# Score, value and up products of a two-block network: the order in which a matmul visits its moving columns

## The reference

```python
def peer_ffn(h, ...):                       # first block, 16384 experts, 8 heads
    ...                                     # routing: the 16 best experts of each head, and their gates
    def chunk(args):
        hc, ec, gc = args
        u = peer_u[ec]
        a = jax.nn.gelu(jnp.einsum("ckd,cd->ck", u, hc)) * gc
        vv = peer_v[ec]
        return jnp.einsum("ck,ckd->cd", a, vv)

def second_block(...):
    ...
    up = causal_dwconv(h2 @ w_up[l], ffn_conv_w[l], ffn_conv_b[l])     # w_up is 1024 x 6144
    gate_h, val_h = jnp.split(up, 2, axis=-1)
    x = x + (jax.nn.gelu(gate_h, approximate=True) * val_h) @ w_down[l]
```

## Time and profile before

| | |
|---|---|
| median of the runs | 1597.97 us |
| the runs | 1597.45 and 1598.48 us |
| span of the profiled execution, first to last instruction | 1595.2 us |
| TensorE matmul busy (PE) | 1583.0 us, 99% |
| weight loads busy (PEld) | 1493.5 us, 94% |
| VectorE, ScalarE, GpSimd busy | 1071.3, 884.2, 885.8 us |
| mean granted TensorE clock | 0.999 |
| DMA | 277.03 MB, mean 174 GB/s |

### The profile page before, as it was taken

One profiled execution on the slowest core, in us unless ns is written; L12 is line 12 of the kernel. 1 busy time (PEld: TensorE's weight loads), 2 busy tenths in 40 slices (PEclk: granted clock), 3 DMA queues, 4 the chain that ended last, 5 costly groups with the idle time before them and its releaser, 6 DMA issues.

```text
span 1595.2 us, 33476 instructions
## 1 busy us (share of the span) xinstructions
PE 1583.0 (99%) x12568; PEld 1493.5 (94%) x12568; DVE 1071.3 (67%) x1867; ACT 884.2 (55%) x1251; POOL 885.8 (56%) x413
## 2 busy tenths in 40 slices
PE   9999999999999999999999999999999999999998
PEld 8999899999999999998888888889999999999998
DVE  7998643779933777778888666776937383455521
ACT  6557766454454444444444445457676654666653
POOL 8786468868886000000000244457876689888886
PEclk9999999999999999999999999999999999999999
DMA  6565346555555555555555666666543356666653
GB/s 222 171 191 154 106 132 187 186 175 190 188 184 186 171 171 171 172 169 171 179 178 166 215 190 194 195 189 185 172 148 106 109 177 185 188 190 187 191 187 119
DMA packets 86218, 277.03 MB, mean 174 GB/s; under 512 B 11233, under 2 KB 18161, under 8 KB 86129
## 3 DMA queue, kind: packets, MB, share of 16 engines
q1 hardware_dynamic: 85712, 274.76, 54.9%
q0 software_dynamic: 272, 1.05, 0.2%
q10 hardware_dynamic: 144, 0.00, 0.0%
HBM read 274.73 MB, written 1.05 MB: 173 GB/s over the span
## 4 chain that ended last, share of the span: by engine, by line
PE 93%; issue 2%; DVE 2%; POOL 1%; ACT 1%; DMA 0%; SPq 0%; DVEq 0%; ACTq 0%; POOLq 0%
PE gemm L679 36%; PE gemm L982 22%; PE gemm L684 18%; PE aux L1268 4%; PE gemm L813 3%; PE aux L962 2%; POOL w_lo L462 1%; PE gemm L700 1%; PE gemm L725 1%; PE gemm L1268 1%; PE aux L932 0%; PE gemm L799 0%; ACT w_hi L1364 0%; PE gemm L706 0%; PE gemm L742 0%
## 5 line engine op out<-in xcount | busy, mean ns | idle before, releaser
L462 POOL TENSOR_TENSOR w_lo<-raw,w_hi 128x1024 fp32r<-128x1024 f32 (+1 forms) x330 | 791.7, 2407 | 294.7 <-ACT w_hi L1364 285.6
L1364 ACT ACTIVATE w_hi<-raw 128x1024 fp32r<-128x1024 f32 (+1 forms) x492 | 515.8, 1050 | 575.5 <-PE gemm L679 324.0
L679 PE MATMUL gemm<-h_lo,w_hi 128*128 128x256 f32 x2144 | 294.3, 279 | 0.0
L679 PE MATMUL gemm<-h_hi,w_hi 128*128 128x256 f32 x2096 | 293.3, 282 | 0.4 <-ACT w_hi L1364 0.3
L684 PE MATMUL gemm<-h_hi,w_lo 128*128 128x256 f32 x2096 | 288.6, 280 | 1.4 <-POOL w_lo L462 0.9
L679 PEld LDWEIGHTS gemm<-h_lo,w_hi 128*128 128x128 f32 x2144 | 268.9, 188 | 0.3 <-issue 0.2
L679 PEld LDWEIGHTS gemm<-h_hi,w_hi 128*128 128x128 f32 x2096 | 264.0, 188 | 3.3 <-issue 1.6
L462 DVE TENSOR_TENSOR w_lo<-raw,w_hi 128x1024 fp32r<-128x1024 f32 x162 | 196.6, 1222 | 104.3 <-ACT w_hi L1364 103.7
L684 PEld LDWEIGHTS gemm<-h_hi,w_lo 128*128 128x128 f32 x2096 | 262.8, 188 | 3.5 <-POOL w_lo L462 2.2
L982 PE MATMUL gemm<-w_hi,act_parts 128*128 128x512 f32 x1008 | 250.9, 391 | 0.4 <-ACT act_parts L1565 0.4
L982 PEld LDWEIGHTS gemm<-w_hi,act_parts 128*128 128x128 f32 x1008 | 188.0, 188 | 39.0 <-issue 0.5
(11 more groups left out here) (436 smaller groups left out, 2065.6 us busy)
## 6 DMA issues: line engine op xcount, KB each, us to landing
raw<-in_w_u SPq DMA_DIRECT2D x128, 512.0 KB, 3.6
raw<-in_w_ev SPq DMA_DIRECT2D x128, 512.0 KB, 3.7
raw<-in_w_up SPq DMA_DIRECT2D x48, 512.0 KB, 4.3
raw<-in_w_gate SPq DMA_DIRECT2D x24, 512.0 KB, 3.8
raw<-in_w_down SPq DMA_DIRECT2D x24, 512.0 KB, 4.0
raw<-in_w_conv_in SPq DMA_DIRECT2D x16, 512.0 KB, 4.6
raw<-in_w_peer_q SPq DMA_DIRECT2D x16, 512.0 KB, 3.5
raw<-in_w_branch SPq DMA_DIRECT2D x24, 288.0 KB, 2.9
```

The lines of the kernel that those rows point to most:

```text
L462: eng.tensor_tensor(w_lo[v][:, 0:n], raw[c.raw][v][:, 0:n], w_hi[v][:, 0:n], ALU.subtract).then_inc(lo_ready[v], 1)
L679: mm = pe.matmul(out, w[:, k, :], act_part[:, k, :], start=(n == k == 0), stop=False)
L1364: act.activation(w_hi[v][:, 0:n], raw[c.raw][v][:, 0:n], ACT.Copy).then_inc(hi_ready[v], 1)
```

## The change

Four new things stand ahead of the products. `ordered(tile, groups, run)` cuts the columns into `groups` equal stretches and visits a run of `run` columns from each stretch in turn. `strided(tile, groups, run)` visits every `groups`-th run first, then the ones behind them, and so on. A run is never shorter than 4 columns, which is 16 bytes. `column_order(c)` finds the order of a chunk by its name and its place in the round, and gives back the columns unchanged for every other chunk. `turn` is put around the moving operand and the output of the matmul alike, so that each column still gets its own sum.

```diff
+        def ordered(tile, groups, run):
+            if groups == 1:
+                return tile
+            return tile.rearrange("p (g j c) -> p j g c", g=groups, c=run)
+
+        def strided(tile, groups, run):
+            return tile.rearrange("p (j g c) -> p g j c", g=groups, c=run)
+
+        SCORE_ORDER = (lambda x: x, lambda x: ordered(x, 2, 4), lambda x: strided(x, 2, 4), lambda x: ordered(x, 2, 8))
+        VALUE_ORDER = (lambda x: ordered(x, 2, 4), lambda x: ordered(x, 4, 4), lambda x: ordered(x, 2, 16), lambda x: x)
+        UP_ORDER = (lambda x: ordered(x, 4, 8), lambda x: ordered(x, 2, 64), lambda x: ordered(x, 8, 4), lambda x: strided(x, 4, 4))
+
+        def column_order(c):
+            for name, orders in (("u", SCORE_ORDER), ("up", UP_ORDER), ("ev", VALUE_ORDER)):
+                first = plan[name][0].index
+                if first <= c.index < first + len(plan[name]):
+                    return orders[(c.index - first) % BANKS]
+            return lambda x: x
@@ product_tile
+                turn = column_order(c)
...
-                        mm = pe.matmul(out, w[:, k, :], act_part[:, k, :], start=(n == k == 0), stop=False)
+                        mm = pe.matmul(turn(out), w[:, k, :], turn(act_part[:, k, :]), start=(n == k == 0), stop=False)
...
-                    mm = pe.matmul(out, w[:, k, :], x[0][:, k, :], start=False, stop=(k == steps - 1))
+                    mm = pe.matmul(turn(out), w[:, k, :], turn(x[0][:, k, :]), start=False, stop=(k == steps - 1))
@@ expert_values
+                turn = column_order(c)
...
-                                mm = pe.matmul(gemm[2 * half + tt][:, :], a[:, c.raw, v, tt * P:(tt + 1) * P],
-                                               w[v][:, half * (D // 2):(half + 1) * (D // 2)],
+                                mm = pe.matmul(turn(gemm[2 * half + tt][:, :]), a[:, c.raw, v, tt * P:(tt + 1) * P],
+                                               turn(w[v][:, half * (D // 2):(half + 1) * (D // 2)]),
```

## The result

The changed kernel takes 1645.23 us (1644.97 and 1645.49) against 1597.97: ratio 1.0296, 95% interval 1.0279 to 1.0314. That is 47.3 us slower, where I had forecast 6 us faster.

The account below looks back on a forecast made before the run. TensorE, always busy, bounds the kernel: matmul distance times number of matmuls. Changes of distance at the turned places summed to -6.1 us, from 1595.2 to 1589.1, plus 2.8 us around the span: forecast 1592 us, range 1575 to 1655.

Parts of the forecast that it names:

- no cover was used up: In u, GpSimd needs 4.84 us for a chunk's remainders, of 5.6 us, so TensorE's gain or loss arrives whole.
- I take zero for a jump: In all turned places a jump inside the columns costs nothing; at 1.67 ns, 281 thousand jumps would cost 469 us.
- The meetings with the weight load: In float32r matmuls, moving stream and weight load wanting one 128-byte residue cost 1.67 ns; four now, 6.7 ns.
- my ten terms: Changes of matmul distance at the turned places of u, ev and up, counted in meetings; sum -6.1 us.
- u's place 2: In u, every second group, then the others: about 6 meetings against four, +3.3 ns x 768, +2.6 us.
- up's place 2: In up, eight stretches in turn, all of one residue: 6 meetings, +3.3 ns x 288, +1.0 us.
- Up's place 3: In up, every fourth group: 8 meetings, +6.7 ns, +1.9 us; it should be the slowest in up.
- the four pairs: Operand pairs in u, query product and by_token (twice): 116 to 118.8 ns by their place difference modulo 128 bytes.
- Order doesn't matter: All turned products: stalls come from how fast float32r columns are read, weights shift them 1.5 ns; 1598 us, chance 0.27.
- the in-step rival: u's and ev's halves in turn, 4 columns, always meet the weights: 28 meetings more, +46.7 ns, above 1653 us; chance 0.08.
- A residue twice in a row: In u, ev and up, groups following one of their own residue pay 1.67 ns each: +171 us, 1769 us; chance 0.10.
- The output: Turned products: jumping writes into PSUM fall to half rate, 217 and 433 ns a matmul, +583 us, 2181 us; chance 0.03.

Follow-up runs that it names:

- the bare streams: Separate kernels computing nothing of the reference: TensorE alone runs streams of 32 matmuls with nothing to wait for; contiguous 256 columns took 116.7 ns each.
- one order for all: Kernel before the change, with each fourth group of 16 bytes in every product of 256 moving columns, value products as they lie: 1580.3 us, ratio 0.988.

## Why the prediction was wrong, point by point

- What bounds the kernel: right. PE was full before and after, the clock stood at its upper level, no wait came in, and the loss is the number of matmuls times the growth of their distance.
- The change adds no instruction and no wait, and no cover was used up: right. The count of matmuls is the same, TensorE's waits are those of before, and the run without the value orders comes out at the sum.
- **"I take zero for a jump"**: this is the step that failed. The reason given was that a contiguous stream changes its 16-byte group as often. It is the distance to the next group that has a price. Halves in turn, 4 columns, have 64 jumps for 10.0 ns, so 0.16 ns each, 128 for 23.7 in ev, 0.19; four stretches in ev 0.32 each; ev's place 2 with 32 jumps 0.42. These lie between my two bounds, 0 and 1.67, and I set the sum at the lower one; only every 4th group in up, with 64 jumps for -1.8 ns, lies below it. In all, the 281 thousand jumps that I had counted at nothing came with 48 us.
- **The meetings with the weight load**: wrong as the source of the sum. Of my ten terms two have the right sign and a size within 6 ns (u's place 2 and up's place 2); the others miss by sign or kind. Up's place 3, which I had as the slowest of up, was the only one that got faster. The reading of the earlier trace rows holds within this kernel: over the whole trace the four pairs stand 117.0, 118.1, 118.5 and 117.0 ns apart. As a rule it fell, because in the bare streams 114.0 and 118.3 ns have the same difference of 112 bytes. And I took all 8 ns of extra for such meetings. With a quarter of the weight columns a contiguous stream still takes 116.6 to 120.0 ns, so most of them are not.
- "Order doesn't matter" fell, and with it the Trainium skill's rule in "TensorE: Matmul & The Clock Gate", Part 2, in its strict form. The weight load does act on the moving stream: 64 bytes past the weights a matmul takes 113.3 ns with 128 weight columns and 120.0 with 32, eight stretches in turn 127.2 and 116.7, and with both operands on one residue it takes 240 ns where 217 is the least.
- The measured time lies in my range of 1575 to 1655 us by luck. What reached above 1600 was the in-step rival with its chance of 0.08; to a slower kernel I had given 0.21 in all. That rival gave 1653 us, near to the 1645 measured, but not for its reason: it has +46.7 ns in u's place 1 and ev's place 0 and nothing in ev's place 1, which paid the most.
- A residue twice in a row: fell as priced, with eight stretches in turn and 32 weight columns (116.7 ns). The turned places whose neighbours are of one residue did pay, but for halves in turn 0.16 ns each and not 1.67.
- The output: fell, output alone is 1602 us. The slowing that the Trainium skill gives for any non-contiguous pattern in "PSUM — Partial Sum Buffer", Specifications (TRN2), didn't show for runs of four columns or more: with the output alone turned, bare streams took 116.7 to 117.8 ns, contiguous 116.7.
- The rule of the Trainium skill, "SBUF — State Buffer", Specifications (TRN2), which I let stand for the sum: all orders of float32r had four hits on a line of 16 bytes, and they took 113.6 to 160 ns. Two hits on a line may be needed; they were not enough here.

Still open: which structure of SBUF gives these prices (the repeat after 256 bytes, and 96 the worst of all constant steps), why the price of eight stretches, and part of that of 512 columns, goes with the weight load, why one and the same stream can stand 120.0 or 117.4 ns apart, why ev's unchanged place 3 stood 1.7 ns higher behind the turned ones (and 227.0 once the value orders were out), and why 113.3 ns of the best place don't show in the kernel.

## What to carry to other kernels

Where float32r matmuls run back to back, the order of the moving columns is a knob of its own, down to single groups of 16 bytes: here one order for all took 1.2% off and a mix of orders added 3%. Measure each order in a bare stream on a line of its own, dozens in a run of 300 us; for eight of the ten turned orders these numbers carried into the kernel within half a nanosecond, for the other two, in up, they were off by 1.0 and 1.8 ns; they didn't carry for the place of a contiguous operand, and only in part for 512 columns by every 4th group. Where a step can't be bounded but by ends 470 us apart, a zero in the sum wants a row of its own; none of mine showed a jump.

## What the runs showed of the hardware that I had not expected

- A float32r stream pays for the distance between the 16-byte groups that it visits: 115.6 ns for 256 columns with a group each 144 bytes, 126.7 each 128, 133.3 each 80, 160.0 each 96. For two stretches in turn it repeats after 256 bytes, and the multiples of 256 are among the dearest (126.7; 528 bytes apart as well).
- bfloat16 in groups of 16 bytes and full float32 pay nothing for the orders tried (109.1 and 215.8 ns), but bfloat16 with a step of 96 bytes pays the same 160.0 ns.
- Visiting every 4th group is faster than going straight on: 114.8 ns at 32 and at 96 bytes past the weights, where contiguous columns take 116.7 and 119.9. At 64 bytes it is slower, 115.1 against 113.3.
- The output's order into PSUM, in runs of four columns, costs at most 1.1 ns of 117 (output alone turned: 116.7 to 117.8 ns; the whole kernel 1602.3 against 1598.2 us, one run each).
- The same float32r stream can settle at two distances: 120.0 ns in one kernel and 117.4 in another, with the same operands.
